# A quarter of the value table as a dense product beside the gathers

## What is computed

```python
q = (xc @ w_q).reshape(TOKEN_CHUNK, N_PEER_HEADS, 2, PEER_HALF)
s1 = einsum('chd,hnd->chn', q[:, :, 0], keys1); s2 = einsum('chd,hnd->chn', q[:, :, 1], keys2)
v1, i1 = lax.top_k(s1, 16); v2, i2 = lax.top_k(s2, 16)
cand = (v1[..., :, None] + v2[..., None, :]).reshape(TOKEN_CHUNK, 8, 256)
top, pos = lax.top_k(cand, 16)
e = take_along_axis(i1, pos // 16) * N_KEYS + take_along_axis(i2, pos % 16)   # N_KEYS = 128
g = softmax(top)
act = gelu(einsum('chkd,cd->chk', u_tab[e], xc))
out = einsum('chkd,chk->cd', v_tab[e], g * act)
```

## Time and profile before

| | |
|---|---|
| runs, us | 2651.66, 2647.88, 2651.38; median 2651.38 |
| profiled execution, span | 2649.7 us, 20755 instructions |
| busy | PE 1935.9 (73%), DVE 1974.5 (75%), POOL 1048.4 (40%), ACT 572.0 (22%) |
| HBM read | 884.13 MB |
| gather queue (q0) | 580.95 MB, 53.2% of 16 engines' span |
| SP's queue (q1) | 282.87 MB, 28.7% |

### The profile page before, as it was taken

One profiled execution on the slowest core, in us unless ns is written; L12 is line 12 of the kernel. 1 busy time (PEld: TensorE's weight loads), 2 busy tenths in 40 slices (PEclk: granted clock), 3 DMA queues, 4 the chain that ended last, 5 costly groups with the idle time before them and its releaser, 6 DMA issues.

```text
span 2649.7 us, 20755 instructions
## 1 busy us (share of the span) xinstructions
PE 1935.9 (73%) x7656; PEld 1329.2 (50%) x7656; DVE 1974.5 (75%) x2446; ACT 572.0 (22%) x863; POOL 1048.4 (40%) x641
## 2 busy tenths in 40 slices
PE   8999999894007777777774000049999999899997
PEld 5877568554002222222221000049878887788886
DVE  6886897978995765544446999999874689877666
ACT  3054010100000000100001000023433443544343
POOL 0000003556784655445545888840165650000000
PEclk9999999997559999999998555569999999999998
DMA  9673879999999999999999999998953459677552
GB/s 379 258 256 141 334 272 404 388 420 422 410 422 422 421 422 421 421 422 421 422 421 422 385 422 421 422 367 297 356 207 113 162 191 366 276 297 290 203 195 108
DMA packets 123508, 887.60 MB, mean 335 GB/s; under 512 B 13840, under 2 KB 14352, under 8 KB 16528
## 3 DMA queue, kind: packets, MB, share of 16 engines
q0 software_dynamic: 79776, 580.95, 53.2%
q1 hardware_dynamic: 39888, 282.87, 28.7%
q10 hardware_dynamic: 3744, 22.47, 2.2%
HBM read 884.13 MB, written 2.10 MB: 334 GB/s over the span
## 4 chain that ended last, share of the span: by engine, by line
PE 42%; DMA 25%; POOL 17%; DVE 12%; issue 4%; ACT 1%; DVEq 0%; ACTq 0%; SPq 0%; POOLq 0%
PE psum L835 21%; POOL W L716 11%; DMA W<-in_peer_v,W 10%; POOL early_rows L716 5%; DMA early_rows<-in_peer_v,W 5%; PE psum L953 4%; DMA W<-in_peer_u,W 4%; DMA early_rows<-in_peer_u,W 3%; PE psum L791 3%; PE psum L767 3%; PE psum L1111 3%; DVE split L1919 2%; DVE W L2267 1%; DVE early_rows L2267 1%; DMA ring<-in_w_even 1%
## 5 line engine op out<-in xcount | busy, mean ns | idle before, releaser
L835 PE MATMUL psum<-split,hi 128*128 128x512 f32 x1664 | 514.7, 390 | 2.4 <-DVE split L1919 2.4
L2267 DVE CUSTOM_DVE_ANT_0 W<-W,XN 128x2048 f32<-128x2048 f32 x148 | 336.2, 2291 | 200.7 <-DMA W<-in_peer_u,W 197.4
L1111 PE MATMUL psum<-W,HT 128*128 128x512 f32 x616 | 286.3, 609 | 267.6 <-ACT HT L1563 169.8
L716 POOL DMA_INDIRECT W<-in_peer_v,W x173 | 318.5, 1841 | 175.2 <-PE psum L1111 141.8
L1345 ACT ACTIVATE split<-ring 128x1024 fp32r<-128x1024 f32 x272 | 282.0, 1057 | 407.7 <-PE psum L835 287.5
L2267 DVE CUSTOM_DVE_ANT_0 early_rows<-early_rows,XN 128x2048 f32<-128x2048 f32 x108 | 245.2, 2291 | 135.8 <-DMA early_rows<-in_peer_u,W 135.4
L835 PEld LDWEIGHTS psum<-split,hi 128*128 128x128 f32 x1664 | 311.5, 188 | 68.0 <-issue 2.7
L1919 DVE TENSOR_TENSOR split<-ring,split 128x1024 fp32r<-128x1024 f32 x206 | 247.1, 1225 | 124.1 <-ACT split L1345 123.0
L1111 PEld LDWEIGHTS psum<-W,HT 128*128 128x128 f32 x616 | 112.4, 192 | 441.1 <-issue 296.7
L716 POOL DMA_INDIRECT W<-in_peer_u,W x148 | 213.1, 1440 | 178.2 <-DVE W L2267 89.4
L693 POOL TENSOR_TENSOR split<-ring,split 128x1024 fp32r<-128x1024 f32 x66 | 172.2, 2635 | 220.1 <-ACT split L1345 220.0
(11 more groups left out here) (376 smaller groups left out, 3104.4 us busy)
## 6 DMA issues: line engine op xcount, KB each, us to landing
ring<-in_ada SPq DMA_DIRECT2D x54, 1024.0 KB, 6.2
ring<-in_odd SPq DMA_DIRECT2D x48, 1024.0 KB, 5.5
XN<-in_ada POOLq DMA_DIRECT2D x19, 1024.0 KB, 7.0
ring<-in_w_out SPq DMA_DIRECT2D x16, 1024.0 KB, 6.0
ring<-in_pq SPq DMA_DIRECT2D x16, 1024.0 KB, 9.0
ring<-in_c_v SPq DMA_DIRECT2D x16, 1024.0 KB, 8.3
ring<-in_c_k SPq DMA_DIRECT2D x16, 1024.0 KB, 8.2
ring<-in_w_even SPq DMA_DIRECT2D x16, 1024.0 KB, 7.1
```

The source lines that it names most:

```text
L716: nc.gpsimd.indirect_dma_start(row, None, t["peer_" + table], bass.IndirectOffsetOnAxis(ap=EIDX[:, c:c + 1], axis=0),).then_inc(full, 16)
L835: m = nc.tensor.matmul(dst, lhs, rhs, start=(k == 0 and b == 0 and not (features and i % 2)), stop=(k == KD - 1 and b == 2 and not (featur ...
L1111: m = nc.tensor.matmul(o[c], DIAG[j % DIAGS], row[:, 512 * c:512 * c + 512], start=(j == 0), stop=(j == P - 1))
L2267: V.tensor_tensor_reduce(out=row, in0=row, in1=xn3[:, tt, :], scale=1.0, scalar=0.0, op0=ALU.mult, op1=ALU.add, accum_out=PACT[:, c:c + 1])\
```

## The change

The experts whose first key is 96 or more (`e >= 96 * 128`, 32 keys of 128 experts, a quarter of the table) are taken out of the value gathers and computed in another way, for both tiles:

- Value gathers get a bounds check at 96 * 128 - 1, with entries beyond it left out; their weights in `PACT` are set to zero, while the whole weights stand in `PGATE`.
- For each tile PE turns the keys and the weights of all choices (`turn_keys`), so that choices stand on the partitions and tokens in the columns; ACT copies them (`keys_evac`). For each group of 8 tokens DVE writes one-hots of the second key (128 wide) and of the first key (32 wide, times the weight) in `hot`; PE multiplies them, one call of 32 columns for each token (`spread`), which gives the weight of each of the 4096 experts; ACT copies two groups at once into `SPREAD`. There are 16 groups for each tile.
- For each of the 32 keys SP loads 128 rows of the value table in order, 1 MB, into the ring, and PE multiplies the spread weights of both tiles with it, 8 calls (`dense`), adding tile 0 to `vacc` and tile 1 to four other banks `vden`.
- 13 of the 128 rows of tile 1 (28, 36, ... 124) are done on PE with diagonals as tile 0's are, in front of keys 4, 6, ... 28; DVE does the other 115.
- `ROW_LIST` puts the first 8 `u` rows of tile 1 ahead of the first `v` row, and 8 `v` rows of tile 1 between the last of tile 0.
- DVE adds `vacc` and `vden` to `x3` at the end; before, `vacc` was added ahead of the rows of tile 1. POOL's `split_lo` for the first pieces stands behind all gathers.

```diff
+LEAD = 8
+ROW_LIST = [("u", 0, j) for j in range(P)] + [("u", 1, j) for j in range(LEAD)]
+for _j in range(P - LEAD):
+    ROW_LIST += [("v", 0, _j), ("u", 1, LEAD + _j)]
+for _j in range(LEAD):
+    ROW_LIST += [("v", 0, P - LEAD + _j), ("v", 1, _j)]
+ROW_LIST += [("v", 1, _j) for _j in range(LEAD, P)]
...
+DENSE = 32
+FIRST_DENSE = NKEY - DENSE
+HOTS, HOT_TOKENS = 16, 8
+ADD_ROWS = [28 + 8 * _k for _k in range(13)]
+VEC_ROWS = [_j for _j in range(P) if _j not in ADD_ROWS]
...
+    def dense_slots(self):
+        for i in range(DENSE):
+            self.slot["dense", i, 0] = len(self.loads)
+            self.loads.append(("dense", i, 0, 2048))
+            if i < DENSE - 1:
+                self.used += 1
+                self.release.append((("slot_used", self.used),))
+            else:
+                self.release.append((self.full(self.unit["vden", 3]),))
...
-                if (table, tt, j) == ("v", 1, AHEAD_ROW):
-                    split_lo(*LAT[0], 0, AHEAD)
...
+                else:
+                    nc.gpsimd.indirect_dma_start(row, None, t["peer_v"], at, bounds_check=NKEY * FIRST_DENSE - 1,
+                                                 oob_is_err=False).then_inc(full, 16)
+            split_lo(*LAT[0], 0, AHEAD)
...
+            def spread(tt, g):
...
+                pe.wait_ge(sem("hot_ready"), 2 * n + 2)
+                for i in range(HOT_TOKENS):
+                    at = DENSE * (HOT_TOKENS * (g % 2) + i)
+                    m = nc.tensor.matmul(u[:, at:at + DENSE], HOT2[n % 2][:, i, :], HOT1[n % 2][:, i, :],
+                                         start=True, stop=True)
...
+            def dense(i):
+                sl = slot_of("dense", i, 0)
+                for tt in range(TT):
+                    for c in range(4):
+                        m = nc.tensor.matmul(o[tt][c], SPREAD[tt][:, i, :], sl[:, 512 * c:512 * c + 512],
+                                             start=(tt == 1 and i == 0), stop=(i == DENSE - 1))
+                        if i == DENSE - 1:
+                            close(m, (("vacc", "vden")[tt], c))
+                if i < DENSE - 1:
+                    m.then_inc(sem("slot_used"), 1)
+            for j in range(P):
+                add_row(0, j, j)
+                if j == 56:
+                    turn_keys(0)
+                if j >= 66 and (j - 66) % 3 == 0 and (j - 66) // 3 < HOTS:
+                    spread(0, (j - 66) // 3)
+                if j == 123:
+                    turn_keys(1)
+            for g in range(HOTS):
+                spread(1, g)
+            o.append([open_unit(("vden", c)) for c in range(4)])
+            pe.wait_ge(sem("spread_done"), TT)
+            for i in range(DENSE):
+                if i >= 4 and i % 2 == 0 and i // 2 - 2 < len(ADD_ROWS):
+                    n = i // 2 - 2
+                    add_row(1, ADD_ROWS[n], P + n)
+                dense(i)
...
+            def hot(tt, g):
...
+                if n >= 2 and n % 2 == 0:
+                    dve.wait_ge(sem("hot_used"), n // 2)
+                elif n >= 2:
+                    wait_unit(dve, (("spread", (n - 2) // HOTS), (n - 2) % HOTS // 2))
...
+                TT_(HOT2[n % 2], key2.to_broadcast(two), const("iota").unsqueeze(1).to_broadcast(two), ALU.is_equal)\
+                    .then_inc(sem("hot_ready"), 1)
+                seq(TT_(HOT1[n % 2], key1.to_broadcast(one),
+                        const("iota", FIRST_DENSE, NKEY).unsqueeze(1).to_broadcast(one), ALU.is_equal))
+                TT_(HOT1[n % 2], HOT1[n % 2], weight.to_broadcast(one), ALU.mult).then_inc(sem("hot_ready"), 1)
...
+            for g in range(HOTS):
+                hot(0, g)
+                dots(1, 72 + 3 * g, 75 + 3 * g)
+            split_keys(1)
+            dots(1, 72 + 3 * HOTS, P)
+            dots_done(2 * P)
+            row_weights(2, P, 2 * P)
+            dve.wait_ge(sem("weights_ready"), 6)
+            for n, j in enumerate(VEC_ROWS):
+                if 2 <= n < 2 + HOTS:
+                    hot(1, n - 2)
+                row, full, value = row_place(ROW_AT["v", 1, j])
+                dve.wait_ge(full, value)
+                STT(x3[:, 1, :], row, PACT[:, P + j:P + j + 1], x3[:, 1, :], ALU.mult, ALU.add)\
+                    .then_inc(sem("row_used"), 1)
```

More of the change, by code:

```diff
@@ L149 @@
 _at = 0
-for _name, _n in (("ident", 128), ("upto", 128), ("zeros", 128), ("from", 128), ("ones", 128), ("iota", 16),
+for _name, _n in (("ident", 128), ("upto", 128), ("zeros", 128), ("from", 128), ("ones", 128), ("iota", 128),
                   ("freq", 32)):
@@ L315, in make_plan @@
     p.gemm("c_k", 2, 4, 2, 2048)
+    vacc, vden = [("vacc", c) for c in range(4)], [("vden", c) for c in range(4)]
     p.units("vacc", 4)
+    p.keep(vacc)
+    for tt in range(TT):
+        p.place(("wT", tt))
+        p.units(("spread", tt), HOTS // 2)
+    p.units("vden", 4)
+    p.dense_slots()
+    p.keep(vden)
+    for c in range(4):
+        p.give_back([vden[c], vacc[c]])
     p.units("x2T", 8)
@@ L1103, in _, with add_row @@
             feature_gemm("c_k", 2, ht)
-            o = [open_unit(("vacc", c)) for c in range(4)]
-            for j in range(P):
-                row, full, value = row_place(ROW_AT["v", 0, j])
-                pe.wait_ge(sem("diag_ready"), j + 1)
+            o = [[open_unit(("vacc", c)) for c in range(4)]]
+            def add_row(tt, j, n):
+                row, full, value = row_place(ROW_AT["v", tt, j])
+                pe.wait_ge(sem("diag_ready"), n + 1)
                 pe.wait_ge(full, value)
@@ L2335, in _ @@
[L2335 to L2352 removed]
+                for tt, name in enumerate(("vacc", "vden")):
+                    wait_unit(dve, (name, c))
+                    give(TT_(x3[:, tt, a], bank((name, c)), x3[:, tt, a], ALU.add), (name, c))
```

160 lines of the change are left out of this document (104 added, 56 removed).

## The result

The changed kernel takes 2675.34 us, the median of four runs (2668.51 to 2681.32), against 2651.52 for the kernel before on the same chip. The ratio is 1.0092, with an interval of 1.0075 to 1.011: slower. The forecast was 2636. The profiled execution is the slowest of the four runs (2681.32 us, 6 above the median). It has a span of 2679.5 us, 29.8 more than before's; x can be turned at 1786.6 us against 1757.4, 29.2 later, so again everything is decided ahead of that point (E). The prediction put E at 1742. The 44.6 us between them are those of this execution; by the medians the forecast was 39.5 us too low.

What follows compares the result with a forecast made beforehand. DMA was taken to bound the expert stage at 2.487 us a row; tile 0's end at 1382, 66 us of one-hots and the dense part gave E 1742 against 1757.4, plus 1.5 behind it: 2636 us, range 2605 to 2692.

Steps and rivals of the forecast that it cites:

- step 3: Dense part with tile 1's rows: DMA sets steps of 20.6 us for two keys and eight rows; E at 1742.
- the skip is free: Value gathers: a skipped entry costs nothing, so they take 1.818 and 1.878 us instead of 2.487.
- Step 1: Up to the end of tile 0: pairs of 4.305 us set by DMA, plus unevenness; tile 0 ends at 1382.
- I take 2%, 11 us, as the windows overlap and a lagging engine catches up: Pair stage: loss to uneven skips over the DMA engines taken as 11 us, between 0 and 45.
- is anything else slower than 4.305?: Pair stage: check of DVE, PE, ACT and POOL against DMA's 4.305 us a pair; PE's up to 15 us taken as nothing.
- Step 2: One-hots of tile 1, after tile 0: 66 us, with about 37 us of idle DMA; dense part starts at 1448.
- With 4% for uneven skips on the gathers: Dense part: uneven skips lengthen the DMA step from 20.0 to 20.6 us; bounds 0 and 13%.
- in which DMA brings 10 more rows: Start of dense part: keys 0 to 3 take 27.5 us, while DMA brings 10 more rows and 4 keys.
- The end: Behind E: bank adds at the end and paired transposes add 1.5 us; POOL's moved subtractions are done at about E.
- Rival (b): Pair stage and dense part: each window of gathers waits for its fullest engine; total 2686 us, slower; chance 0.28.
- Rival (a): Pair stage and dense part: even skips, no loss to unevenness; E 1725, total 2618 us; chance 0.17.
- (d): Dense part: PE sets the end with DMA ahead; E 1702, total 2596 us; chance 0.07.

Runs made afterwards that it cites:

- e1: Kernel before with only the bounds check on its value gathers, skipped entries not computed in any other way; 2581.63 us, ratio 0.9736.
- e8: Changed kernel with constant indices in the value gathers, every fourth entry skipped, dealt out evenly; 2644.16 us, ratio 0.9971.
- e9: Kernel before with constant indices in the value gathers, 25.0% of entries skipped, always on the same 32 partitions; 2646.58 us, ratio 0.998.
- e15: e14 with constant, evenly dealt skips in the value gathers; 2632.43 us, ratio 0.9927.
- e12: Changed kernel with ten places for last gathers, PE's tile 1 rows at 20, 28, ... 116, top-k blocks cut in three between dot rows; 2654.44 us, 1.001.
- e13: e12 with three of the last rows of tile 1 (120, 122, 124) given to PE; 2647.36 us, ratio 0.9984.
- e14: e13 with PE's rows of tile 1 put somewhat earlier among the keys; 2660.08 us, ratio 1.0036.
- e6: Changed kernel without the searches of tile 1's last three top-k groups, which use stale indices; 2663.7 us, ratio 1.0046.
- e7: Changed kernel without tile 1's one-hots and spread matmuls, tile 0's spread weights used for both tiles; 2633.16 us, ratio 0.9923.
- e11: e8 with all ten places for the last gathers instead of eight; 2641.28 us, ratio 0.996.

## Why the prediction was wrong

The mechanism of unevenness was seen, its size was not; the clock and the chain of one place in step 3 were not seen. E came 44.6 us after the forecast: 16.8 of them at the first key, 3.1 up to row 28, 22.2 in the twelve steps, 2.1 behind row 124.

- *That the skip is free* was right (e1: 70 us gained; e8: 418 to 419 GB/s beside a quarter skipped).
- *Step 1 failed in the term "I take 2%, 11 us, as the windows overlap and a lagging engine catches up".* A lagging engine does not catch up, since its partitions are its own (e9) and DMA is the bound. The count for each engine gives 17 us (533 against 516), and e8 and e15 show some 17. "The descriptor swizzle", the section of the Trainium skill's "DMA: Bandwidth & Descriptors" that the prediction cited and set aside, ties each engine to eight fixed partitions. e9 bears the tie out for four engines together, and the 6.5% that the prediction worked out with it was the better term. The question "is anything else slower than 4.305?" was put for the one-hots' pairs alone, and there it was right: gathers 136 to 376 take 546.4 us in the changed kernel and 546.6 in e1, which has no one-hots and no spread calls. So PE's bound in these 48 pairs (up to 15 us, taken at nothing) was rightly at nothing, and e15, with the spread calls, moves 417 GB/s through the whole stage. The question was not put for the three top-k blocks of 14.3 us before them. They stood in before too, with the same waits of POOL; there 20.8 us of gathers in flight covered them, while here the gathers in flight are shorter, and the rate fell to 395. They cost tile 0's end some 6 us: it came at 1393.6, 1391.1 and 1393.3 in e12, e13 and e14 and at 1392.3 in e6, against 1398.3. In all the stage lost 30 us to the full rate: 17 to the fullest engine, 7 to the blocks, and 6 that stay with both repaired and whose cause is open. The prediction had allowed 11.
- *Step 2* was right: 64.7 us for 66, its start being 18 us late, and 42 us when its one-hots go (e7) where 37 of idle DMA were forecast.
- *Step 3 failed in "With 4% for uneven skips on the gathers", in "in which DMA brings 10 more rows" and in "granted clock 1.0".* At the fullest engine's 7.7% over the tile the step is 15.0 x 1.077 + 5.0 = 21.2 us, not 20.6. And beside it stands the one place that rows 28 + 8n share: row 36's gather waits for row 28, so the ten rows' lead that made 11.25 steps of 12 cannot be had, and each late row stops POOL's queue. A late row is also a slow one: after the waits the granted clock was 0.5, and rows took 5.1 to 6.7 us, not 3.6. Since the next gather goes out only behind the row, this time enters the step, 12 us over the twelve steps (in e8, by the same count, 5). No run takes the clock away alone, so how much of these 12 the end would give back is not shown. The cold start that the prediction priced at 2.5 us and left out of its sum is the 3 us ahead of row 28: the first key began at a granted clock of 0.5. Measured without the first quick steps: 21.9 in the changed kernel (one quick step, 17.2), 21.3 with ten places (two), 20.1 with even skips (two). Together 12 x 21.5 = 258 us against 236 forecast. With even skips the place costs at most 3 us of the time, with uneven ones 10: what makes rows late and what makes a late row dear work on each other.
- *The end* was right: nothing behind E changed by more than 1 us.
- *Rival (b)* had the time (2686 against 2675) and nearly the cause. It counted the fullest engine of each window; the fullest engine of the whole tile is the smaller and better number. It stood in the range, and had 0.28.
- *Rival (a)*, even skips, is e8's case, and was itself too low: 2644 for 2618. Of these 26 us 6 are the lower skip share of tile 0 and 7 the blocks; the rest is not taken apart.
- *(d)* falls: PE waits for rows all through step 3.

The whole: 84 us of DMA time were taken out net, and the changed kernel leaves the DMA short of its full rate by some 116 us between row 0 and E: 30 to the end of tile 0, 35 in the one-hot stage, 50 behind it, of which 22 lie behind 1757 us (108 GB/s over 30 us), when the last gathers have landed and PE ends the keys. By the runs, even skips and ten places together give 34 us (e11), 39 with the lower skip share; 42 go with the one-hot stage (e7), 6 to 7 with the blocks. These were not taken away all at once, so they need not add up. e13 takes back 28 us by order and places alone, with nothing left out.
